# Token blocks interleaved element by element in the stationary tiles, and 128 unused bytes behind each half of hT

## What is computed

```python
h = _rms_norm(x, attn_norm_g[l])
proj = h @ w_in[l]                       # 2048 x 13312: three mixers' inputs and three gates
o_da  = _diff_attention(...)             # 8 heads, causal
o_ret = _retention(...)                  # 8 heads, in chunks
o_mem = _memory_attention(...)           # 4 heads over 256 memory tokens
merged = (jax.nn.sigmoid(g_da) * (o_da @ w_o_da[l])
          + jax.nn.sigmoid(g_ret) * (o_ret @ w_o_ret[l])
          + jax.nn.sigmoid(g_mem) * (o_mem @ w_o_mem[l]))
x = x + merged @ w_out[l]
hf = _rms_norm(x, ffn_norm_g[l])
x = x + (jax.nn.silu(hf @ w_ffn_gate[l]) * (hf @ w_ffn_up[l])) @ w_ffn_down[l]   # d_ff 5632
```

## Time and profile before

| | |
|---|---|
| runs, median of 2 | 1627.67 us (1627.34 to 1628.01) |
| profiled execution, first to last instruction | 1625.4 us |
| PE busy | 1618.2 us, 7373 matmuls |
| PE weight loads busy | 1339.3 us, 7373 |
| DVE busy | 1271.1 us |
| ACT busy | 908.2 us |
| POOL busy | 80.6 us |
| granted TensorE clock | 1.00 of full speed |
| DMA | 341.35 MB, mean 210 GB/s |

### The profile page before, as it was taken

The page is one execution under the profiler, slowest core; times in us unless marked ns, Lnnn a source line. Parts: engine busy times, 40 slices in busy tenths (PEclk is TensorE's granted clock), DMA queues, the critical chain, the costliest instruction groups (busy, mean ns, idle before and its releaser), DMA issues.

```text
span 1625.4 us, 20227 instructions
## 1 busy us (share of the span) xinstructions
PE 1618.2 (100%) x7373; PEld 1339.3 (82%) x7373; DVE 1271.1 (78%) x1325; ACT 908.2 (56%) x989; POOL 80.6 (5%) x73
## 2 busy tenths in 40 slices
PE   9999999999999999999999999999999999999999
PEld 7888888888888888888888888888888888888887
DVE  5565545589777777777975589999999999999995
ACT  6654454555555554445554465656655665656653
POOL 0000000000011100000000000100100100100101
PEclk9999999999999999999999999999999999999999
DMA  9876555556554555566675756868868868868866
GB/s 339 278 214 194 157 180 175 174 179 220 179 166 162 164 172 168 174 188 199 202 245 182 249 166 207 252 211 248 246 212 250 249 208 249 244 220 240 253 211 178
DMA packets 178007, 341.35 MB, mean 210 GB/s; under 512 B 11793, under 2 KB 16401, under 8 KB 177169
## 3 DMA queue, kind: packets, MB, share of 16 engines
q1 hardware_dynamic: 167056, 319.45, 60.4%
q0 software_dynamic: 10880, 20.97, 7.1%
HBM read 317.31 MB, written 2.10 MB: 197 GB/s over the span
## 4 chain that ended last, share of the span: by engine, by line
PE 90%; issue 6%; DVE 1%; DMA 1%; POOL 1%; ACT 1%; SPq 0%; DVEq 0%; ACTq 0%; POOLq 0%
PE acc L1582 43%; PE at L1664 9%; PE at L1666 9%; PE at L1665 9%; PE acc L1666 5%; PE acc L1664 5%; PE acc L1665 5%; PE at L1582 3%; PE at L1604 2%; POOL rstd L480 1%; PE at L1642 0%; PE at L1657 0%; DMA raw<-in_w_mem_kv 0%; DMA raw<-in_w_in 0%; DVE w_lo L929 0%
## 5 line engine op out<-in xcount | busy, mean ns | idle before, releaser
L929 DVE TENSOR_TENSOR w_lo<-raw,w_hi 128x1024 fp32r<-128x1024 f32 x319 | 386.6, 1222 | 239.6 <-ACT w_hi L507 235.4
L507 ACT ACTIVATE w_hi<-raw 128x1024 fp32r<-128x1024 f32 x319 | 337.1, 1060 | 360.9 <-PE acc L1582 300.3
L1582 PE MATMUL acc<-w_hi,hT_hi 128*128 128x512 f32 x752 | 297.6, 396 | 0.0
L1582 PE MATMUL acc<-w_hi,hT_lo 128*128 128x512 f32 x752 | 293.1, 390 | 0.0
L1582 PE MATMUL acc<-w_lo,hT_hi 128*128 128x512 f32 x752 | 293.0, 390 | 0.0
L857 ACT ACTIVATE f_hi<-sum 128x2048 fp32r<-128x2048 f32 x60 | 115.3, 1922 | 121.2 <-DVE sum L1461 118.0
L1582 PEld LDWEIGHTS acc<-w_hi,hT_hi 128*128 128x128 f32 x752 | 141.2, 188 | 30.9 <-issue 1.3
L1582 PEld LDWEIGHTS acc<-w_hi,hT_lo 128*128 128x128 f32 x752 | 141.2, 188 | 29.7
L1582 PEld LDWEIGHTS acc<-w_lo,hT_hi 128*128 128x128 f32 x752 | 141.3, 188 | 28.4
L1582 PE MATMUL acc<-w_hi,oT_hi 128*128 128x512 f32 x384 | 151.2, 394 | 1.5 <-DVE oT_lo L955 1.4
L1582 PE MATMUL acc<-w_hi,oT_lo 128*128 128x512 f32 x384 | 149.6, 390 | 0.0
(11 more groups left out here) (349 smaller groups left out, 2658.1 us busy)
## 6 DMA issues: line engine op xcount, KB each, us to landing
raw<-in_w_in SPq DMA_DIRECT2D x208, 512.0 KB, 3.8
f_raw<-in_w_ffn_down SPq DMA_DIRECT2D x88, 512.0 KB, 4.8
f_raw<-in_w_ffn_gate SPq DMA_DIRECT2D x80, 512.0 KB, 3.9
f_raw<-in_w_ffn_up SPq DMA_DIRECT2D x80, 512.0 KB, 5.0
proj<-down POOLq DMA_DIRECT2D x40, 512.0 KB, 6.4
raw<-in_w_mem_kv SPq DMA_DIRECT2D x32, 512.0 KB, 6.2
raw<-in_w_out SPq DMA_DIRECT2D x32, 512.0 KB, 3.7
raw<-in_w_o_mem SPq DMA_DIRECT2D x16, 512.0 KB, 5.0
```

The lines of the kernel that those rows point to most:

```text
L507: act.activation(w_hi[:, s % RING], raw[:, s % RING], ACT.Copy).then_inc(hi_done, 1)
L929: v.tensor_tensor(w_lo[:, s % RING], raw[:, s % RING], w_hi[:, s % RING].bitcast(F32), ALU.subtract).then_inc(lo_done, 1)
L1582: e = pe.matmul(dst, a[:, k0 + k, tok], w[:, s % RING, k, :], start=first and k == 0 and n == 0, stop=last and k == 1 and n == 2)
```

## The change

Tokens are interleaved in every stationary tile of hT, aT and the combined blocks: number 2m + t of a group of 256 is token m of block t. A stationary tile is then every second number, `t::2`, 8 bytes apart. The host lays `x_t` out so. The transposes of `turn_columns` and `turn_acts` write every second number of PSUM. DVE makes the combined blocks with reads and writes of every second number, into [2, 128, 2] instead of [4, 128]. Two tiles of 32 numbers that nothing uses stand behind hT_hi and behind hT_lo. The tiles oT_hi and oT_lo and all their products stay as they are, and so do the moving operands. The number, the order and the waits of the instructions stay the same on every engine.

```diff
         hT_hi = sb("hT_hi", [P, KD, TOK], F32R)
+        sb("gap_hi", [P, 32])
         hT_lo = sb("hT_lo", [P, KD, TOK], F32R)
+        sb("gap_lo", [P, 32])
...
-            ("cmb_lo", [P, NS, 4, P], F32R), ("cmb_hi4", [P, 2, 4, P], F32R))
+            ("cmb_lo", [P, NS, 2, P, 2], F32R), ("cmb_hi4", [P, 2, 2, P, 2], F32R))
...
                     if s == 2:
-                        a11, a12, a21, a22 = (p_whole[:, k, t * P:(t + 1) * P] for t in range(TB) for k in range(2))
-                        v.tensor_tensor(p_mixed[:, 3], a11, a21, ALU.subtract).then_inc(p_cmb, 1)
-                        step(v.tensor_tensor(p_mixed[:, 0], a22, a21, ALU.subtract), p_cmb, i * 5 + 3)
...
+                        a11, a12, a21, a22 = (p_whole[:, k, t::TB] for t in range(TB) for k in range(2))
+                        v.tensor_tensor(p_mixed[:, 1, :, 1], a11, a21, ALU.subtract).then_inc(p_cmb, 1)
+                        step(v.tensor_tensor(p_mixed[:, 0, :, 0], a22, a21, ALU.subtract), p_cmb, i * 5 + 3)
...
             def three_passes(s, hi, lo, k0, p, k, t, first, last):
-                tok = slice(t * P, (t + 1) * P)
+                tok = slice(t, TOK, TB) if hi is hT_hi else slice(t * P, (t + 1) * P)
...
                     for t in range(TB):
-                        e = turn(at[:, k % 4, t * P:(t + 1) * P], src[:, t, c0 + k * P:c0 + (k + 1) * P])
+                        e = turn(at[:, k % 4, t:TOK:TB], src[:, t, c0 + k * P:c0 + (k + 1) * P])
...
             def block_a(t, k):
-                return hT_hi[:, k, t * P:(t + 1) * P], hT_lo[:, k, t * P:(t + 1) * P]
+                return hT_hi[:, k, t::TB], hT_lo[:, k, t::TB]
...
                 def combined(c):
-                    return p_cmb_hi[:, i, c, :], p_cmb_lo[:, i, c, :]
+                    return p_cmb_hi[:, i, c // 2, :, c % 2], p_cmb_lo[:, i, c // 2, :, c % 2]
...
                     for t in range(TB):
-                        c0 = (k % 2) * 256 + t * P
-                        e = turn(dst[:, k // 2, c0:c0 + P], gt[:, t, k * P:(k + 1) * P])
+                        c0 = (k % 2) * TOK
+                        e = turn(dst[:, k // 2, c0 + t:c0 + TOK:TB], gt[:, t, k * P:(k + 1) * P])
...
             def combined(i, c):
-                return cmb_hi[:, i, c, :] if i < 4 else cmb_hi4[:, i - 4, c, :], cmb_lo[:, i, c, :]
+                hi = cmb_hi[:, i] if i < 4 else cmb_hi4[:, i - 4]
+                return hi[:, c // 2, :, c % 2], cmb_lo[:, i, c // 2, :, c % 2]
...
                 for k in range(4):
-                    e = product(at[:, 2 * (n % 2) + t, :], hi[:, k, t * P:(t + 1) * P],
-                                lo[:, k, t * P:(t + 1) * P], *whole(f, p, u, k), k == 0, k == 3)
+                    e = product(at[:, 2 * (n % 2) + t, :], hi[:, k, t::TB], lo[:, k, t::TB], *whole(f, p, u, k),
+                                k == 0, k == 3)
...
-        "x_t": inputs["x"][0].T, "mem_t": inputs["mem"][0].T,
+        "x_t": inputs["x"][0].T.reshape(D, TB, P).transpose(0, 2, 1).reshape(D, TOK), "mem_t": inputs["mem"][0].T,
```

More of the change, by code:

```diff
@@ L151, in program @@
                                             ("hi1", quad, F32R), ("sum0", quad, F32R if stage else F32), ("hi0", quad, F32R),
-                                            ("pad2", [P, 10 * NCOL], F32), ("cmb_hi", [P, 4, 4, P], F32R),
-                                            ("pad3", [P, 10 * NCOL], F32), ("cmb_lo", [P, 4, 4, P], F32R)):
+                                            ("pad2", [P, 10 * NCOL], F32), ("cmb_hi", [P, 4, 2, P, 2], F32R),
+                                            ("pad3", [P, 10 * NCOL], F32), ("cmb_lo", [P, 4, 2, P, 2], F32R)):
                         early[stage, name] = overlay.enter_context(nc.sbuf_tensor(f"p_{name}_{stage}", shape, dt))
@@ L161, in program @@
                     for t in range(TB):
-                        for name, shape, dt in (("r_cmb", [P, 4, 4, P], F32R), ("r_sum", [P, 4, NCOL], F32R if stage else F32),
+                        for name, shape, dt in (("r_cmb", [P, 4, 2, P, 2], F32R), ("r_sum", [P, 4, NCOL], F32R if stage else F32),
                                                 ("r_hi", [P, 4, NCOL], F32R), ("r_act", [P, 2 * NCOL], F32)):
@@ L166, in program @@
                 for name, shape, dt in (("r_rows", [P, 4, 4, P], F32), ("r_whole", [P, 2, TOK], F32),
-                                        ("r_mixed", [P, 4, P], F32)):
+                                        ("r_mixed", [P, 2, P, 2], F32)):
                     branch[0, name, 0] = overlay.enter_context(nc.sbuf_tensor(name, shape, dt))
@@ L182, in program @@
             ("rows_t0", rows_tile, F32), ("f_raw2", quad_tile, F32), ("sum0", quad_tile, F32), ("act_t0", act_tile, F32),
-            ("rows_t1", rows_tile, F32), ("sum1", quad_tile, F32), ("cmb_hi", [P, 4, 4, P], F32R),
+            ("rows_t1", rows_tile, F32), ("sum1", quad_tile, F32), ("cmb_hi", [P, 4, 2, P, 2], F32R),
             ("act_t1", act_tile, F32),
-            ("cmb_lo", [P, NS, 4, P], F32R), ("cmb_hi4", [P, 2, 4, P], F32R))
+            ("cmb_lo", [P, NS, 2, P, 2], F32R), ("cmb_hi4", [P, 2, 2, P, 2], F32R))
         with ExitStack() as ffn:
@@ L226, in program @@
         p_whole = p_sum[1][:, 0, :].rearrange("p (k c) -> p k c", k=2)
-        p_mixed = p_sum[1][:, 1, :].rearrange("p (c m) -> p c m", c=4)
+        p_mixed = p_sum[1][:, 1, :].rearrange("p (a m b) -> p a m b", a=2, b=2)
         p_out = [[proj[:, :, (2 * r + c + 8) * NCOL:(2 * r + c + 9) * NCOL] for c in range(2)] for r in range(2)]
@@ L825, in _ @@
                     act.wait_ge(cmb_f, 5)
-                    act.activation(cmb_hi[:], sums[1][:].rearrange("p q (c m) -> p q c m", c=4),
+                    act.activation(cmb_hi[:], sums[1][:].rearrange("p q (a m b) -> p q a m b", a=2, b=2),
                                    ACT.Copy).then_inc(cmb_split, 1)
@@ L829, in _ @@
                     act.wait_ge(cmb_f4, 5)
-                    act.activation(cmb_hi4[:], sums[0][:, 2:4].rearrange("p q (c m) -> p q c m", c=4),
+                    act.activation(cmb_hi4[:], sums[0][:, 2:4].rearrange("p q (a m b) -> p q a m b", a=2, b=2),
                                    ACT.Copy).then_inc(cmb_split, 1)
@@ L1054, in _ @@
                     if s == 2:
-                        a11, a12, a21, a22 = (p_whole[:, k, t * P:(t + 1) * P] for t in range(TB) for k in range(2))
-                        v.tensor_tensor(p_mixed[:, 3], a11, a21, ALU.subtract).then_inc(p_cmb, 1)
-                        step(v.tensor_tensor(p_mixed[:, 0], a22, a21, ALU.subtract), p_cmb, i * 5 + 3)
-                        step(v.scalar_tensor_tensor(out=p_mixed[:, 1], in0=p_mixed[:, 0], scalar=-1.0, in1=a11,
+                        a11, a12, a21, a22 = (p_whole[:, k, t::TB] for t in range(TB) for k in range(2))
+                        v.tensor_tensor(p_mixed[:, 1, :, 1], a11, a21, ALU.subtract).then_inc(p_cmb, 1)
+                        step(v.tensor_tensor(p_mixed[:, 0, :, 0], a22, a21, ALU.subtract), p_cmb, i * 5 + 3)
+                        step(v.scalar_tensor_tensor(out=p_mixed[:, 0, :, 1], in0=p_mixed[:, 0, :, 0], scalar=-1.0, in1=a11,
                                                     op0=ALU.mult, op1=ALU.subtract), p_cmb, i * 5 + 4)
-                        v.tensor_tensor(p_mixed[:, 2], a12, p_mixed[:, 1], ALU.add).then_inc(p_cmb, 1)
+                        v.tensor_tensor(p_mixed[:, 1, :, 0], a12, p_mixed[:, 0, :, 1], ALU.add).then_inc(p_cmb, 1)
                     if s == 8:
@@ L1297, in _ @@
                     if s == 2:
[L1298 to L1301, removed]
+                        a11, a12, a21, a22 = (r_whole[:, k, t::TB] for t in range(TB) for k in range(2))
+                        v.tensor_tensor(r_mixed[:, 1, :, 1], a11, a21, ALU.subtract).then_inc(r_cmb, 1)
+                        step(v.tensor_tensor(r_mixed[:, 0, :, 0], a22, a21, ALU.subtract), r_cmb, i * 5 + 3)
+                        step(v.scalar_tensor_tensor(out=r_mixed[:, 0, :, 1], in0=r_mixed[:, 0, :, 0], scalar=-1.0, in1=a11,
                                                     op0=ALU.mult, op1=ALU.subtract), r_cmb, i * 5 + 4)
-                        v.tensor_tensor(r_mixed[:, 2], a12, r_mixed[:, 1], ALU.add).then_inc(r_cmb, 1)
+                        v.tensor_tensor(r_mixed[:, 1, :, 0], a12, r_mixed[:, 0, :, 1], ALU.add).then_inc(r_cmb, 1)
                     if s == 6:
@@ L1410, in combine @@
                                      hT_lo[:, 2 * q0:2 * q1, :].bitcast(F32), ALU.add), done, 1)
[L1411 to L1415, removed]
+                a11, a12, a21, a22 = (pairs[:, :, k, t::TB] for t in range(TB) for k in range(2))
+                v.tensor_tensor(mixed[:, :, 1, :, 1], a11, a21, ALU.subtract).then_inc(done, 1)
+                step(v.tensor_tensor(mixed[:, :, 0, :, 0], a22, a21, ALU.subtract), done, 3)
+                step(v.scalar_tensor_tensor(out=mixed[:, :, 0, :, 1], in0=mixed[:, :, 0, :, 0], scalar=-1.0, in1=a11, op0=ALU.mult,
```

(8 more changed lines are left out.)

## The result

| | before | changed |
|---|---|---|
| median (range) of 2 runs | 1627.67 us (1627.34 to 1628.01) | 1652.71 us (1652.02 to 1653.40) |
| profiled execution, first to last instruction | 1625.4 us | 1650.2 us |
| ratio of the runs, 95% interval | | 1.0154 (1.0125 to 1.0184) |

The predicted time was 1627, the range 1608 to 1645; the measured time lies outside, on the side of slower. It is within 2% of before, which had been given a chance of 0.84, and the two pairs of runs lie far apart, so that the direction isn't in doubt.

The account below looks back on a forecast made before the run. PE was taken to bound the kernel through the price of one matmul. All terms were taken as 0, so the profiled 1625.4 us stayed and the runs' median, 2.3 us above, gave 1627 us, range 1608 to 1645.

Parts of the forecast that it names:

- What bounds the kernel: PE, busy 1618.2 of 1625.4 us; no other engine holds it up, so the price of one matmul decides.
- the count of 5,445 matmuls: Products on hT, aT and combined blocks that the change touches; 1 ns each would be 5.4 us.
- PSUM writes of every second number: The 120 transposes for hT and aT: taken as 0, or 13.1 us more if such writes take twice as long.
- rival (c): PSUM writes with gaps in the transposes cost double: 1641 us, chance 0.07.
- DVE's combinations: Small gapped operations making combined blocks: even doubled, hidden beside products; taken as 0, upper bound 4.4 us.
- rival (b): On hT, aT and combined blocks, gapped loads outlast their room: 278 us more at 2.5 times, 1905 us; chance 0.05.
- The 13 ns above 213: Each 227 ns product step's excess over 512 columns at 2.4 GHz; attributed to moving operands, not to weight loads.
- rival (a): Weight loads do interfere now; products fall from 227 to 216 ns on all 5,445, 58 us, 1570 us; chance 0.14.
- the part on weight loads: Loads of every second number for hT, aT and combined blocks: taken as 0, between minus 5.4 and plus 5.4 us.
- the gaps: 128 bytes behind hT_hi and hT_lo shift tiles' addresses: 0 with no interference to remove, otherwise within the same bound.
- The rows with and without a load: Products on hT_lo and the last product: 388 ns without a load beside, 389 with one, so interference is 1 ns.
- alone or not: Comparing products with and without a load beside: if loads took array time, one alone would finish 11 to 13 ns sooner.

Follow-up runs that it names:

- m2: No layer, only groups of 24 matmuls with more distances, few weights, or bf16; one weight takes 231.3 ns, bf16 215.8 ns per matmul.
- e2: The changed kernel without its two gaps, so interleaving alone; 1660.97 us, ratio 1.0207 to the kernel before.
- e1: The kernel before with the two gaps of 128 bytes alone, no interleaving; 1641.15 us, ratio 1.0085.
- e3: The kernel before with gaps of 256 bytes behind hT_hi and hT_lo, tiles contiguous; 1627.63 us, ratio 1.000.
- m1: No layer, only groups of 24 matmuls at various distances and steps; at distance 0, 226.7 ns at step 1, 233.3 at step 2.
- e5: The kernel before, contiguous, with one gap of 128 bytes behind hT_lo only; 1648.98 us, ratio 1.0132.

## Why the prediction was wrong

**Right.** What bounds the kernel, the count of 5,445 matmuls, and that everything hangs on a few ns per step. PSUM writes of every second number cost nothing (0.87 us for 8, as expected at 0), so rival (c) is out. The Trainium skill ("Advanced Engine Details and Errata", Memory Cachelines) says that non-contiguous PSUM patterns slow matmuls significantly; for these transposes, one number each 0.85 ns, the measurement says otherwise. DVE's combinations are hidden. Gapped loads take 193 ns instead of 188 and products on gapped tiles 231 to 233 ns, nowhere near the 278 of rival (b), which is out. The 13 ns above 213 don't come from the number of weights read: m2 has more than 13 with one weight, and bf16, with a load of 128 weights beside each matmul, has 2.5. No product fell to 216 ns, so rival (a) is out as a forecast. Its premise, that distance matters between what is loaded and what streams, came true with the opposite sign.

**The step that failed** is the part on weight loads: "Between, today's interference of 1 ns may vanish (minus 5.4 us) or double [...] I take 0, as the nearest rows, products with and without a load, differ by 1 ns only", and after it, on the gaps, "With no interference to remove, this is 0". Measured, the two terms together are plus 25 us, where each had been bounded by 5.4. By themselves the step of two costs 33.6 us (e2) and the gaps 13.8 (e1). The rows with and without a load were used for something that they don't bear: how a product's time reacts when the addresses move. Every product of the trace before, whatever its tile, has step 1 and a distance that is a multiple of 512 bytes; the prediction itself says that all tiles start at one remainder and that no load has a gap. At one point no row can show a slope. That point turned out to be the least of all that were tried: from 226.7 ns a product goes up to between 231 and 234 for distances of 8 to 160 bytes, and to 233.3 for step 2 at distance 0. "On two kinds of stationary tile at different addresses the step is the same" looked like evidence that addresses don't matter; the two kinds differ by multiples of 512 bytes only.

A second sign stands in the changed traces. The product before the wait, at 433.22 us, again has no weight load beside it, and its duration is 397 ns, not 388; this is the reading of the earlier trace rows. In e1, where hT_lo is contiguous and 128 bytes off, it is 401 ns. Groups by line, the changed kernel at 433.45 to 433.5 us, then e1 at 432.56 to 432.6:

```profile
L1583 PE MATMUL acc<-w_hi,hT_lo 128*128 128x512 f32 x1 | 0.4, 397 | 0.0
```
```profile
L1584 PE MATMUL acc<-w_hi,hT_lo 128*128 128x512 f32 x1 | 0.4, 401 | 0.0
```

Of the products on hT and aT with no load beside them, 8 of 11 have a duration of 397 ns in the changed kernel and 3 of 387. In e1 all 11 on hT_lo have 397 to 401, and the one on aT_lo, at distance 0, 388. In e3 all of them have 388. So a product's duration depends on where tiles lie while no load runs beside it, as far as the profile's modelled ends can be trusted. The test "alone or not" could not have ruled out an effect of layout in the first place.

**Sizes.** Both parts of the change enter: interleaving costs 33.6 us by itself, by starts 6.2 ns on each of 5,445 products, and the gaps take 8.3 us back on hT alone (231 instead of 233.3 ns on 3,609 products, 8 us). Why they do is only in part shown. By m1, hT_lo's distance of 128 suits step 2 better (231.5 ns). But most of the gain is on hT_hi (230.8 instead of 233.4 ns, 6.2 us), whose distance of 256 gave 233.3 in m1 as 0 did. There two distances in turn may be what helps; no group at step 2 tried that, so it isn't shown.

**What stays open.** The runs show that a matmul's time depends on the distance (at step 1 modulo 256 bytes; at step 2 not on that alone, 233.3 ns at 0 and 235.7 at 512), on the step of the stationary tile, below 64 bytes on the absolute place, and on the tiles of its neighbours. They don't show what in the chip does it. A cost per weight read is out, since fewer weights didn't help; but with 1 to 96 weights instead of 128 the 226.7 ns at distance 0 become 230 to 232, so the load isn't a bystander. In groups whose matmuls all take the same, the averages are 226.7, 233.3 and 240.0 ns, which at 2.4 GHz are 544, 560 and 576 array steps, multiples of 16. That fits a start that has to wait for a recurring place, but no run tests it.

## What to carry to other kernels

Where a trace holds one setting of a quantity only, such as one distance between operands, it says nothing on other settings; bound the change by a measurement of groups of matmuls, which takes one short run. For fp32r products of 512 columns keep stationary tiles contiguous and put all stationary and moving tiles at one remainder of 256 bytes; in the groups, shifts of both operands by 64, 128, 192 and 256 bytes came back to 226.7 ns, one by 4 bytes cost 11 ns. A spare tile of 128 bytes between two others cost 0.8% here because it moved the rests of hT, a sixth of all stationary tiles, off that remainder (e1), and 1.3% when it moved all of hT (e5).

## What was not expected of the hardware

- A pad of 128 bytes between tiles costs 13.8 us (1.0085), one of 256 bytes nothing (1.000).
- A matmul of 512 fp32r columns with a contiguous stationary tile takes 226.7 to 238 ns by addresses alone, bf16 215.8 at step 1 and 2.
- One weight column instead of 128 doesn't make it quicker (231.3 ns); 384 columns take 173.3, 448 take 206.7 ns.
- One tile at another distance disturbs the product before it: in e1 and in m2 that one goes from 227 to 232.5 ns, and after a change of addresses the times can take ten matmuls to settle.
- A step of four lengthens a weight load from 188 to 309 ns, and the matmul from 226.7 to 235.2 only.
